# Expert outputs scattered inside the following step, another order of the weight refills, and three read-ahead tiles that wait for the first gather, in a hybrid decoder layer on one core

## The reference, cut to what matters

```
out = zeros_like(t)                                     # t: 264 x 1024
for e in range(16):                                     # each token uses 2 experts of one group
    hdn = silu(t @ w_gate_e[e]) * (t @ w_up_e[e])       # 1024 -> 512
    out = out + combine[:, e:e+1] * (hdn @ w_down_e[e]) # 512 -> 1024, combine is 0 for experts not chosen
h = h + out
h = h + (p @ w_ple) * sigmoid(rmsnorm(h, g_ple) @ w_ple_gate)
y = rmsnorm(h, g_final)
```

## Time and profile before

| what | value |
|---|---|
| median of 3 runs | 606.64 us (606.27 to 607.57) |
| the profiled execution: its time, its span from first to last instruction | 605.79 us, 604.1 us |
| PE busy | 543.0 us, 90% of the span |
| DVE busy | 263.2 us, 44% |
| ACT busy | 162.5 us, 27% |
| DMA | 164.21 MB, 272 GB/s over the span |
| mean granted PE clock | 0.957 of full |

### The profile page before, as it was taken

The page is one execution under the profiler, slowest core; times in us unless marked ns, Lnnn a source line. Parts: engine busy times, 40 slices in busy tenths (PEclk is TensorE's granted clock), DMA queues, the critical chain, the costliest instruction groups (busy, mean ns, idle before and its releaser), DMA issues.

```text
span 604.1 us, 7591 instructions
## 1 busy us (share of the span) xinstructions
PE 543.0 (90%) x2743; PEld 351.1 (58%) x2743; DVE 263.2 (44%) x783; ACT 162.5 (27%) x381; POOL 87.6 (15%) x104
## 2 busy tenths in 40 slices
PE   5999999998767778999983999999999999999994
PEld 3888888875545656888771343434343434353782
DVE  1799789413477676101262032414040404040553
ACT  3211211131488683222242010101010101010543
POOL 4000156123144540030000000000000000000000
PEclk9999999998879787999997999999999999999997
DMA  8733444379868858595095399999999999999201
GB/s 339 250 139 141 145 162 167 121 52 236 272 212 255 266 206 314 234 344 237 14 391 189 105 414 423 423 420 422 420 422 420 423 420 422 422 419 422 119 0 72
DMA packets 35755, 164.21 MB, mean 272 GB/s; under 512 B 6456, under 2 KB 12936, under 8 KB 19472
## 3 DMA queue, kind: packets, MB, share of 16 engines
q1 hardware_dynamic: 25104, 139.69, 59.3%
q0 software_dynamic: 6080, 21.80, 11.8%
q10 hardware_dynamic: 4544, 2.37, 1.4%
HBM read 153.43 MB, written 8.26 MB: 268 GB/s over the span
## 4 chain that ended last, share of the span: by engine, by line
PE 78%; DVE 8%; DMA 5%; ACT 4%; issue 3%; SPq 2%; POOL 1%; DVEq 0%; POOLq 0%; ACTq 0%
PE ps L1146 19%; PE ps L922 18%; PE ps L1022 10%; PE ps L1171 10%; PE ps L1208 5%; PE ps L1189 4%; DMA ring<-glu 2%; DVE xraw_s L1422 2%; PE ps L1108 2%; PE ps L913 2%; SPq L374 1%; DMA xbc<-u_rows,slot_tok 1%; DMA ring<-bc_rows 1%; PE ps L1102 1%; PE ps L944 1%
## 5 line engine op out<-in xcount | busy, mean ns | idle before, releaser
L922 PE MATMUL ps<-u,ring 128*128 128x264 f32 x640 | 145.0, 389 | 0.0
L922 PEld LDWEIGHTS ps<-u,ring 128*128 128x128 f32 x640 | 122.6, 192 | 21.6 <-issue 0.4
L1146 PE MATMUL ps<-ring,xraw 128*64 128x512 f32 x480 | 108.4, 605 | 1.1 <-ACT xraw L825 1.1
L1146 PEld LDWEIGHTS ps<-ring,xraw 128*64 128x64 f32 x480 | 33.6, 139 | 65.3 <-issue 63.7
L1171 PE MATMUL ps<-ring,xraw 128*64 128x512 f32 x256 | 57.6, 596 | 5.5 <-ACT xraw L834 5.5
L1627 DVE TENSOR_TENSOR h<-h,ps 128x264 f32<-128x264 f32 x64 | 27.5, 429 | 79.5 <-PE ps L1189 78.6
L1022 PE MATMUL ps<-cat,ring 128*128 128x264 f32 x256 | 60.6, 400 | 1.6 <-DVE cat L1472 1.6
L1022 PEld LDWEIGHTS ps<-cat,ring 128*128 128x128 f32 x256 | 50.4, 198 | 11.5 <-issue 2.4
L596 POOL DMA_INDIRECT xbc<-u_rows,slot_tok x9 | 8.5, 948 | 266.7 <-DVE slot_tok L1586 216.9
L1171 PEld LDWEIGHTS ps<-ring,xraw 128*64 128x64 f32 x256 | 17.8, 137 | 40.1 <-issue 32.0
L522 POOL TENSOR_TENSOR glu<-asg 128x256 f32<-128x256 f32 x8 | 21.4, 2671 | 94.1 <-ACT asg L670 94.1
(11 more groups left out here) (281 smaller groups left out, 610.2 us busy)
## 6 DMA issues: line engine op xcount, KB each, us to landing
ring<-in_w_moe SPq DMA_DIRECT2D x92, 1024.0 KB, 14.6
ring<-in_w_in SPq DMA_DIRECT2D x20, 1024.0 KB, 5.2
ring<-in_w_out SPq DMA_DIRECT2D x8, 1024.0 KB, 6.5
ring<-in_state_s POOLq DMA_DIRECT2D x8, 512.0 KB, 9.5
out_h_s_out<-ring POOLq DMA_DIRECT2D x8, 512.0 KB, 6.2
ring<-in_w_pleg SPq DMA_DIRECT2D x4, 1024.0 KB, 22.2
asg<-acs_rows ACTq DMA_DIRECT2D x8, 256.0 KB, 4.3
glu<-bc_rows POOLq DMA_DIRECT2D x4, 512.0 KB, 6.0
```

The source lines that it names most:

```text
L922: ins = mm(ps[:, BANK[n], 0:T], wv[:, k, q * P:(q + 1) * P], u[:, k, :], start=(k == 0), stop=(k == KD - 1))
L1146: ins = mm(ps[e * CAP:(e + 1) * CAP, gu, :], xg[:, 4 * hf + k, e * CAP:(e + 1) * CAP], wk, start=(hf == 0 and k == 0), stop=(hf == 1 and k ...
```

## The change

Four things are changed in the expert stage.

1. A step's scatter moves into the next step. PE does four of its eight matmuls after the up projection and four after the transposes of `hid`, over banks 3, 4, 7 and 0 (`SC`). DVE adds them behind `hid`. The last step's scatter is done after the loop over banks 5, 6, 7 and 2 (`SC_LAST`), once `xg` has been copied out of banks 5 and 6. One counter `sc_psum` and one `sc_added` replace three of each.
2. The transposes of `selw` move behind the down projection and write bank 2.
3. SP issues the refill of the gate tiles of step 3 (`load_step(2, range(AHEAD), 1)`) before, not after, the refills of the up and down tiles of step 2.
4. The second and the third read-ahead tile, and with them the two half tiles behind them on SP, wait until the first gather has landed (`xgt_loaded`).

The diff, cut to its core:

```diff
-        SC = [7, 2, 1]
-        SC_N = [3, 3, 2]
+        SC = [3, 4, 7, 0]
+        SC_LAST = [5, 6, 7, 2]
...
-            sp.wait_ge(utok_psum, 3)
+            sp.wait_ge(u_stored, 32)
+            sp.wait_ge(xgt_loaded, 16)
             load_ahead(1)
-            sp.wait_ge(u_stored, 32)
             load_ahead(2)
...
+            load_step(2, range(AHEAD), 1)
             load_step(1, range(AHEAD, MOER), 1)
-            load_step(2, range(AHEAD), 1)
             load_step(2, range(AHEAD, MOER), 2)
...
+            def scatter(step, chunks, banks, added):
+                for c in chunks:
+                    if c == 0:
+                        pe.wait_ge(selt_ready, step + 1)
+                    if c % 4 == 0:
+                        pe.wait_ge(ytok_ready[c // 4], step)
+                    if c >= 4:
+                        pe.wait_ge(sc_added, added + c - 3)
+                    mm(ps[:, banks[c % 4], 0:T], ysb[:, c, :], selt, start=True, stop=True).then_inc(sc_psum, 1)
...
-                pe.wait_ge(selw_ready, step)
-                pe.wait_ge(silu_ready, step)
-                for t, (t0, tn) in enumerate(TOK):
-                    ins = tr(ps[:, 0, t0:t0 + tn], selw[0:tn, t, :], ident[0:tn, 0:tn])
-                ins.then_inc(selt_psum, 1)
+                if behind:
+                    pe.wait_ge(silu_ready, step)
+                    scatter(step - 1, range(4), SC, KD * step - 2 * KD)
                 pe.wait_ge(hid_ready, step)
-                pe.wait_ge(sc_added[1], 3 * step - 2)
                 for k in range(4):
                     ins = tr(ps[:, 2, k * P:(k + 1) * P], hid[:, k * P:(k + 1) * P], ident[:, :])
                 ins.then_inc(hidt_psum, 1)
+                if behind:
+                    scatter(step - 1, range(4, KD), SC, KD * step - 2 * KD)
+                    pe.wait_ge(sc_added, KD * step - 2 * KD + 6)
                 pe.wait_ge(hidt_ready, step)
...
+                pe.wait_ge(selw_ready, step)
+                for t, (t0, tn) in enumerate(TOK):
+                    ins = tr(ps[:, 2, t0:t0 + tn], selw[0:tn, t, :], ident[0:tn, 0:tn])
+                ins.then_inc(selt_psum, 1)
                 pe.wait_ge(tok_ready, step + 1)
                 pe.wait_ge(xgt_loaded, 16 * step + 16)
                 turn_rows()
-                pe.wait_ge(selt_ready, step + 1)
-                for c in range(KD):
-                    q = c % 3
-                    if c % 4 == 0:
-                        pe.wait_ge(ytok_ready[c // 4], step)
-                    pe.wait_ge(sc_added[q], SC_N[q] * step - SC_N[q] + 1 + c // 3)
-                    mm(ps[:, SC[q], 0:T], ysb[:, c, :], selt, start=True, stop=True).then_inc(sc_psum[q], 1)
...
-            pe.wait_ge(ytok_ready[1], steps)
-            for q in range(3):
-                pe.wait_ge(sc_added[q], SC_N[q] * steps + 1)
+            pe.wait_ge(xg_ready, steps + 1)
+            pe.wait_ge(sc_added, added)
+            scatter(steps, range(KD), SC_LAST, added)
...
                 v.tensor_tensor(hid, silu_e, ps[:, 1, :], ALU.mult).then_inc(hid_ready, 1)
+                if behind:
+                    if behind > 1:
+                        dve.wait_ge(sc_added, KD * step - 2 * KD)
+                    add_rows(KD * step - 2 * KD, SC)
                 dve.wait_ge(selt_psum, step)
-                v.tensor_copy(selt, ps[:, 0, 0:T]).then_inc(selt_ready, 1)
-                for c in range(KD):
-                    q = c % 3
-                    dve.wait_ge(sc_psum[q], SC_N[q] * step - SC_N[q] + 1 + c // 3)
-                    v.tensor_tensor(h[:, c, :], h[:, c, :], ps[:, SC[q], 0:T], ALU.add).then_inc(sc_added[q], 1)
+                v.tensor_copy(selt, ps[:, 2, 0:T]).then_inc(selt_ready, 1)
```

More of the change, by code:

```diff
@@ L317, in build @@
         ytok_ready = [sem(f"ytok_ready{o}") for o in range(2)]
-        sc_psum = [sem(f"sc_psum{q}") for q in range(3)]
-        sc_added = [sem(f"sc_added{q}") for q in range(3)]
+        sc_psum = sem("sc_psum")
+        sc_added = sem("sc_added")
         sel_steps = sem("sel_steps")
@@ L827, in _ @@
             end = act.value_load(nsteps[0:1, 1:2], min_val=PAIRS + 1, max_val=PAIRS * MAXQ + 1)
-            steps = act.value_load(nsteps[0:1, 0:1], min_val=PAIRS, max_val=PAIRS * MAXQ)
-            last_adds = act.value_load(nsteps[0:1, 2:3], min_val=3 * PAIRS - 1, max_val=3 * PAIRS * MAXQ - 1)
+            added = act.value_load(nsteps[0:1, 2:3], min_val=KD * (PAIRS - 1), max_val=KD * (PAIRS * MAXQ - 1))
             with act.Fori(1, end) as step:
@@ L843, in _ @@
             for c in range(KD):
-                act.wait_ge(sc_added[c % 3], (last_adds if c % 3 < 2 else 2 * steps) + c // 3)
+                act.wait_ge(sc_added, added + c + 1)
                 a.activation(u[:, c, :], h[:, c, :], ACT.Copy, scale=par("g_ple", c)).then_inc(u_ready, 1)
@@ L1124, in _, with expert_step @@
             steps = pe.value_load(nsteps[0:1, 0:1], min_val=PAIRS, max_val=PAIRS * MAXQ)
-            def expert_step(step, landed, gate_tiles):
+            added = pe.value_load(nsteps[0:1, 2:3], min_val=KD * (PAIRS - 1), max_val=KD * (PAIRS * MAXQ - 1))
+            def scatter(step, chunks, banks, added):
[7 more added lines that the diff above has]
+                    mm(ps[:, banks[c % 4], 0:T], ysb[:, c, :], selt, start=True, stop=True).then_inc(sc_psum, 1)
+            def expert_step(step, landed, gate_tiles, behind):
                 pe.wait_ge(xg_ready, step)
@@ L1129, in expert_step @@
                 pe.wait_ge(selt_ready, step)
+                if behind > 1:
+                    pe.wait_ge(sc_added, KD * step - 2 * KD)
                 for gu in range(2):
@@ L1134, in expert_step @@
                         slot_tokens()
-                        pe.wait_ge(sc_added[2], 2 * step - 1)
+                        if behind:
+                            pe.wait_ge(hid_ready, step - 1)
                     for hf in range(2):
@@ L1181, in expert_step @@
                 turn_rows()
[L1183 to L1189 removed]
             early = {j: [ahead[j][:, k, :] for k in range(4)] for j in range(AHEAD - 1)}
             early[3] = [ahead_parts[k // 2][:, k % 2, :] for k in range(4)]
[L1193 to L1194 removed]
+            expert_step(1, lambda j: 16, {}, 0)
+            expert_step(2, lambda j: 32, early, 1)
             with pe.Fori(3, end) as step:
[L1196 to L1200 removed]
+                expert_step(step, lambda j: 16 * step - (16 if j < AHEAD else 0), {}, 2)
+            pe.wait_ge(xg_ready, steps + 1)
+            pe.wait_ge(sc_added, added)
+            scatter(steps, range(KD), SC_LAST, added)
             for j in range(KD):
@@ L1579, in _ @@
             v.tensor_scalar(nsteps[:, 0:1], nr, float(PAIRS), float(PAIRS), ALU.mult, ALU.add)
-            v.tensor_scalar(nsteps[:, 2:3], nr, 3.0 * PAIRS, 3.0 * PAIRS - 1, ALU.mult, ALU.add)
+            v.tensor_scalar(nsteps[:, 2:3], nr, float(KD * PAIRS), float(KD * PAIRS - KD), ALU.mult, ALU.add)
             v.tensor_scalar(nsteps[:, 1:2], nr, float(PAIRS), float(PAIRS + 1), ALU.mult, ALU.add).then_inc(routes, 1)
@@ L1595, in _ @@
             link(v.tensor_tensor(w2, w1, e2, ALU.mult))
-            for q in range(3):
-                dve.sem_inc(sc_added[q], 1)
             dve.sem_inc(selt_ready, 1)
@@ L1600, in _, with add_rows, route_step @@
             end = dve.value_load(nsteps[0:1, 1:2], min_val=PAIRS + 1, max_val=PAIRS * MAXQ + 1)
-            steps = dve.value_load(nsteps[0:1, 0:1], min_val=PAIRS, max_val=PAIRS * MAXQ)
-            with dve.Fori(1, end) as step:
+            added = dve.value_load(nsteps[0:1, 2:3], min_val=KD * (PAIRS - 1), max_val=KD * (PAIRS * MAXQ - 1))
+            def add_rows(base, banks):
+                for c in range(KD):
+                    dve.wait_ge(sc_psum, base + c + 1)
+                    v.tensor_tensor(h[:, c, :], h[:, c, :], ps[:, banks[c % 4], 0:T], ALU.add).then_inc(sc_added, 1)
+            def route_step(step, behind):
                 for t in range(3):
@@ L1621, in _ @@
                 v.tensor_tensor(hid, silu_e, ps[:, 1, :], ALU.mult).then_inc(hid_ready, 1)
+                if behind:
+                    if behind > 1:
+                        dve.wait_ge(sc_added, KD * step - 2 * KD)
+                    add_rows(KD * step - 2 * KD, SC)
                 dve.wait_ge(selt_psum, step)
-                v.tensor_copy(selt, ps[:, 0, 0:T]).then_inc(selt_ready, 1)
-                for c in range(KD):
-                    q = c % 3
-                    dve.wait_ge(sc_psum[q], SC_N[q] * step - SC_N[q] + 1 + c // 3)
-                    v.tensor_tensor(h[:, c, :], h[:, c, :], ps[:, SC[q], 0:T], ALU.add).then_inc(sc_added[q], 1)
-            for q in range(3):
-                dve.wait_ge(sc_added[q], SC_N[q] * steps + 1)
+                v.tensor_copy(selt, ps[:, 2, 0:T]).then_inc(selt_ready, 1)
+            route_step(1, 0)
+            route_step(2, 1)
+            with dve.Fori(3, end) as step:
+                route_step(step, 2)
```

(2 more changed lines are left out.)

## The result

The changed kernel takes 603.1 us, the median of 20 runs (600.16 to 605.98), against 606.67 (603.01 to 611.44) for the kernel before in the same comparison. The ratio is 0.994 with a 95% interval of 0.9917 to 0.9963: faster, by 3.6 us. Forecast were 602.1, from 598.0 to 606.5.

The account below looks back on a forecast made before the run. PE was taken to set the pace, with the slower weight stream living on its lead. Terms -4.3 + 1.56 - 0.92 - 0.9 gave -4.5 us off the median 606.64: 602.1 us, range 598.0 to 606.5.

Parts of the forecast that it names:

- first gather: Ahead of step 1's gate: with the read-ahead held, the gather lands in 4.2 instead of 8.49 us, -4.3.
- wait for the store: Store of the tokens ahead of the first gather: its 2.83 us wait stays, 0; bounds 0 and -2.8.
- clock: PE's turned rows and first gate: the low clock level costs 2.9 us as before, 0; bounds -2.9 and +2.1.
- steps and stall: Expert steps: moved scatter costs +1.56 us together; step 8's down projection loses its wait for weights, -0.92.
- end: Embedding after the last scatter: PE needs only chunk after chunk of `u`, not all adds, -0.9 us.
- the quiet one: The gather of step 2, which flies alone in the earlier profile and lands in 4.2 us.
- the rival's 2.9 us: Rival, chance 0.17: shorter idle keeps PE's clock up, so rows and first gate run at 2.4 GHz, 599.2 us.
- The covers: Between up and down: scatter halves cover the waits for `hid` and `hidt`; the sixth add is seen at 3.98, inside 4.15 us.
- new wait for `xg`: At each step's end, PE waits for ACT's copy once the scatter no longer covers it: +1.28 us a step.
- The stream: Weight loads: refills follow the read-ahead without a gap, then run continuously; step 8's stall goes, 7 us to spare, -0.92.
- the gather did get faster: Rival, chance 0.08, claimed the opposite: 8.49 us is the indirect read itself, so 606.4 us, no change.
- DVE's adds: Rival, chance 0.13: adds hold the down projection from 0.52 us each; at 0.69, +7.1, 609.2 us.

Follow-up runs that it names:

- e2: The changed kernel with the refills back in the old order: 601.17 us, ratio 0.9894 to the kernel before.
- e3: The kernel before with only the held read-ahead and the new refill order, scatter unmoved: 600.45 us, ratio 0.9902 to the kernel before.
- e1: The changed kernel with the read-ahead issued as before, not held for the first gather: 607.75 us, ratio 1.0017 to the kernel before.
- e4: The changed kernel with read-ahead and refill order as before, so the scatter's move alone: 605.93 us, ratio 1.001 to the kernel before.
- e5: The changed kernel plus eight matmuls nobody reads in PE's wait for the first gather: 600.03 us, ratio 0.9873 to the kernel before.
- e6: The changed kernel with ACT's copy to `xg` in two halves, a semaphore each: 597.84 us, ratio 0.9868 to the kernel before.
- e8: e3 plus eight unread matmuls in the gather wait, without PE's wait for all adds ahead of the embedding: 598.36 us, ratio 0.9839 to the kernel before.
- e9: e7 without PE's wait for `selt` ahead of the gate: 594.9 us, ratio 0.9783 to the kernel before.
- e7: The changed kernel with e5's unread matmuls, e6's halved `xg` copy, and `selw` transposes behind the turned rows: 596.56 us, ratio 0.9847 to the kernel before.

## Why the prediction was right, and which terms were off

The forecast of a faster kernel held, by the mechanism it named, and the time came 1.0 us above it. The terms are those of one profile, and there a chance offset helped the sum: the -0.59 of the store, which nothing shows to be an effect of the change, stands against steps that came out 1.0 too long.

| term | predicted | measured in the profiles |
|---|---|---|
| first gather | -4.3 | 8.49 to 4.65: -3.84 |
| wait for the store | 0 | 2.83 to 2.24: -0.59 in this profile |
| clock | 0 | rows 1.95 to 1.90: -0.05; the gate, 9.17 to 9.00, is in the next row |
| steps and stall | +1.56 - 0.92 = +0.64 | second part 230.02 to 231.65: +1.63 |
| end | -0.9 | 4.54 to 3.66: -0.88 |
| sum | -4.5 | 249.52 to 245.78: -3.74 |

**First gather: right, 0.5 too much.** "With the read-ahead held until it lands, the first gather is in the position of the quiet one": 4.65 here, 4.26 and 4.32 in e2 and e3, 4.7 to 4.8 in the others, against 8.94 and 9.57 in e1 and e4, where the read-ahead is free. The one quiet gather that I took the 4.2 from the earlier trace rows was at the low end.

**Store: 0 was right.** Over the profiles its wait is 2.24 to 3.24 where the read-ahead is held (the change, e2, e3, e5, e6, e8, e9) and 2.19 to 2.83 where it isn't (before, e1, e4). The two overlap, so nothing shows the -0.59 to be an effect of the hold. The Trainium skill ("DMA: Bandwidth & Descriptors", Queues, rings and completion order) says that each DMA engine consumes the descriptors of a ring in ring order, and that a later one may still finish its write before an earlier one. The overlap agrees with the first of these; no run here shows the second.

**Clock: right.** It fell after 3.76 us without PE work, as it had after 2.7 in the earlier trace rows. In the seven profiles without the filler PE's idle time is 3.8 to 4.4 us with the read-ahead held and 8.2 to 8.6 without, and the first gate takes 8.87 to 9.00 and 8.97 to 9.93: halving the idle time saved little. That a filler keeps it up (e5) shows that the rival's 2.9 us were there to be had, 2.3 of them in fact, but not by the shorter wait alone.

**Steps: the mechanism was right, the size was off.** The covers held: from step 2 on none of PE's matmuls waits for `hid`, for `hidt` or for the sixth add (step 1, which has no scatter in it, still waits 0.9 for `hid` and 0.7 for `hidt`), whose end near 399.98 is 3.85 behind the end of up, as predicted. The new wait for `xg` came at the place and at nearly the size named (from the turned rows to the gate 2.38, predicted 2.21 + 0.16). Mis-sized were the small terms: the way from up to down is 4.19, not 4.15, and the `selw` transposes hold PE for 0.53, not 0.44: they are busy 0.59 and the turned rows start 0.53 after them, so that 0.06 was to be taken off and not 0.16. Why wasn't tried. A step is 29.00, not 28.85, and 7 x 0.15 = 1.05 us is nearly all of what the second part came out too long (+1.63 against +0.64, with 0.17 given back by the gate).

**The stream: the conclusion held, two of its steps did not.** "From there the stream is continuous" failed: between 360 and 380 it ran at 266 to 421 GB/s, since SP still waits for slots to come free there (13.4 us for one of them, until it issues the next refill at 363.8), and the "7 us to spare" were 1.3. And the stall was credited to the new order of refills, which e2 shows to be worth nothing here: the stall that it was to remove goes for the most part with the moved scatter alone (e4: 0.3 left of 0.92). Why the whole of it went with the unmoved scatter in e3, by the order or by the held read-ahead, wasn't separated.

**The end: right**, -0.88; e8 shows that it needs no moved scatter, only that the wait for all adds goes.

**The rivals.** The clock did not stay up, the gather did get faster. DVE's adds follow each other by 0.44, under the 0.52 from which they would have held the down projection, and the only trace of them is in the weight loads, which wait for them 0.3 us in each of seven steps (total us, times, longest) without an idle time ahead of the down projection:

```profile
PEld ps L1185 <- DVE h L1617: 2.4, 7, 0.3
```

One consequence the forecast left unsaid: the scatter's move, by far the largest edit, costs 1.3 us in this kernel by the profiles (e3 against the change), and the whole gain lies in the few lines of SP's that hold the read-ahead.

## What to carry to other kernels

A small gather that the chain waits for can lie behind bulk transfers that nobody needs yet: look for what is in flight beside it, and hold that until the gather has landed. When work is moved to cover a wait, name what the old place of that work had covered, since a wait of the same size can turn up there, as the copy of `xg` did. And before making an engine faster, work out the bound of the next one over a step: here the weights took 31.1 us a step by the forecast's sum and lived on their lead. A step of 28.36 us still arrived in full with the clock kept up (e7); of the gain of a step of 28.13 with the low clock (e6) and of the last 0.75 us a step (e9), more than half turned into waits for the stream.

## What the runs showed of the hardware

- A gather of 128 rows, 0.52 MB, took 4.3 to 4.8 us with quiet DMA engines and 8.5 to 9.6 beside the read-ahead, where the DMA engines moved 318 to 329 GB/s between 318 and 323 us (before, e1, e4): the bulk transfers about doubled it.
- Eight matmuls without use, 3.72 us in a wait of some 4, kept the granted clock at 1.00 where it had been 0.75 and 0.79, and the stretch from the slot list to the embedding was 2.3 us shorter (e5 against the change).
- In all four profiles with the filler the slot list stands at 315.5 to 316.5 us, in the other seven at 312.8 to 314.5, although the filler is issued behind it. It isn't in the stretches compared above. The shift is older than the filler's own matmuls (319.37 in e5): ACT's line 783 (785 in e6, e7 and e9) already starts at 254.0 to 255.1 in the four and at 251.3 to 253.1 in the seven. What causes it was not tried and stays open.
